# Delta-rule heads with chunks of 128 tokens: a third doubling level of the triangular inverse, half as many steps in the scan of the state

## The reference

```
G = cumsum(g, axis=-1)                                   # within a chunk
decay = exp(where(causal, G[..., :, None] - G[..., None, :], -inf))
lower = where(strict, einsum('nbhcd,nbhsd->nbhcs', kb, k) * decay, 0.0)
sol = triangular_solve(lower + eye(CHUNK), [v * beta, kb * exp(G)])
u, w = sol[..., :DV], sol[..., DV:]
qk = where(causal, einsum('nbhcd,nbhsd->nbhcs', q, k) * decay, 0.0)
q_dec, k_end = q * exp(G)[..., None], k * exp(G[..., -1:] - G)[..., None]

def step(S, inp):                                        # one chunk after another
    v_new = u - w @ S
    o = q_dec @ S + qk @ v_new
    S = exp(G[..., -1]) * S + k_end.T @ v_new
```

## Time and profile before

| | us |
|---|---|
| median of 3 runs | 1446.78 (1440.41 to 1448.28) |
| the profiled execution | 1447.03 |
| its span, first to last instruction | 1445.2 |
| PE busy | 1268.2 (88%) |
| DVE, POOL, ACT busy | 469.6, 322.9, 296.6 |
| mean granted clock of PE | 0.944 of full speed |

### The profile page before, as it was taken

One profiled execution on the slowest core, in us unless ns is written; L12 is line 12 of the kernel. 1 busy time (PEld: TensorE's weight loads), 2 busy tenths in 40 slices (PEclk: granted clock), 3 DMA queues, 4 the chain that ended last, 5 costly groups with the idle time before them and its releaser, 6 DMA issues.

```text
span 1445.2 us, 17309 instructions
## 1 busy us (share of the span) xinstructions
PE 1268.2 (88%) x5997; PEld 715.2 (49%) x5997; DVE 469.6 (32%) x1159; ACT 296.6 (21%) x619; POOL 322.9 (22%) x326
## 2 busy tenths in 40 slices
PE   3989999999997996799898879999999596989875
PEld 1447757766764754233333245666666342333223
DVE  1454555456464126000000144334342610000004
ACT  2323323332432212000010031111111310000001
POOL 0042223123121000333343102231320031323310
PEclk9989999899997997999999989999999798999997
DMA  9855535543564027999999952432410979999982
GB/s 376 338 206 199 220 92 190 199 137 144 215 221 143 24 76 318 398 375 397 380 351 387 370 211 89 128 131 92 143 60 1 388 290 380 388 396 401 424 355 106
DMA packets 91441, 351.79 MB, mean 243 GB/s; under 512 B 28997, under 2 KB 66693, under 8 KB 72464
## 3 DMA queue, kind: packets, MB, share of 16 engines
q0 software_dynamic: 19872, 188.22, 32.0%
q1 hardware_dynamic: 69280, 159.18, 30.2%
q10 hardware_dynamic: 2256, 3.96, 0.7%
HBM read 374.30 MB, written 21.60 MB: 274 GB/s over the span
## 4 chain that ended last, share of the span: by engine, by line
PE 69%; DMA 20%; DVE 5%; issue 2%; ACT 2%; POOL 1%; SPq 1%; POOLq 0%; DVEq 0%; ACTq 0%
DMA slot<-in_w_x,widx 12%; PE bank L1340 10%; PE bank L1901 9%; PE bank L1944 8%; PE bank L712 8%; PE bank L1260 6%; PE bank L807 3%; PE bank L720 2%; PE bank L352 2%; DMA out_d<-wide,lidx 2%; DMA slot<-in_ada_w 2%; PE bank L832 2%; PE bank L769 2%; PE bank L780 2%; PE bank L428 1%
## 5 line engine op out<-in xcount | busy, mean ns | idle before, releaser
L1901 PE MATMUL bank<-slot,wide 128*64 128x512 f32 x1152 | 262.6, 613 | 37.5 <-DMA slot<-in_w_x,widx 37.5
L1901 PEld LDWEIGHTS bank<-slot,wide 128*64 128x64 f32 x1152 | 89.2, 141 | 206.1 <-issue 157.2
L1340 PE MATMUL bank<-wide,slot 128*128 128x384 f32 x512 | 169.5, 488 | 3.4 <-DMA slot<-in_mlstm_w 2.0
L1944 PE MATMUL bank<-slot,wide 128*64 128x512 f32 x608 | 138.0, 607 | 21.8 <-DMA slot<-in_w_x,widx 13.7
L1340 PEld LDWEIGHTS bank<-wide,slot 128*128 128x128 f32 x512 | 95.6, 190 | 67.3 <-DMA slot<-in_mlstm_w 2.3
L712 PE MATMUL bank<-wide,slot 128*128 128x384 f32 x384 | 126.0, 488 | 0.2 <-DMA slot<-in_gdn_w 0.2
L2056 POOL DMA_INDIRECT slot<-in_w_x,widx x98 | 98.9, 1010 | 57.9 <-POOL widx L2053 41.0
L2019 DVE TENSOR_TENSOR wide<-wide,bank 128x512 f32<-128x512 f32 x19 | 13.1, 687 | 300.7 <-PE bank L1901 300.7
L712 PEld LDWEIGHTS bank<-wide,slot 128*128 128x128 f32 x384 | 72.3, 190 | 55.5 <-issue 5.9
L1944 PEld LDWEIGHTS bank<-slot,wide 128*64 128x64 f32 x608 | 46.4, 139 | 101.3 <-issue 85.2
L1260 PE MATMUL bank<-wide,slot 128*128 128x384 f32 x256 | 87.2, 503 | 7.4 <-DMA slot<-in_w_out 6.7
(11 more groups left out here) (316 smaller groups left out, 1662.7 us busy)
## 6 DMA issues: line engine op xcount, KB each, us to landing
slot<-in_ada_w SPq DMA_DIRECT2D x24, 2048.0 KB, 13.3
slot<-in_w_x SPq DMA_DIRECT2D x12, 2048.0 KB, 19.3
slot<-in_gdn_w SPq DMA_DIRECT2D x9, 2048.0 KB, 14.5
slot<-in_mlstm_w SPq DMA_DIRECT2D x16, 1024.0 KB, 7.0
wide<-rows_d SPq DMA_DIRECT2D x32, 384.0 KB, 4.4
slot<-in_w_out SPq DMA_DIRECT2D x2, 4096.0 KB, 15.3
slot<-inverse_d SPq DMA_DIRECT2D x16, 384.0 KB, 4.1
slot<-out_d SPq DMA_DIRECT2D x6, 1024.0 KB, 7.2
```

The source lines that it names most:

```text
L1340: mm = nc.tensor.matmul(bank[:, PROJ_BANK[s], 0:T], slot[:, 0, (s * KD + k) * P:(s * KD + k + 1) * P], hnT[:, k, :], start=(k == 0), stop= ...
L1901: mm = nc.tensor.matmul(bank[lanes[lane], m, :], xgT[:, k * P + lane * CAP:k * P + (lane + 1) * CAP], w[lane][:, k, :], start=(k == 0), st ...
L1944: mm = nc.tensor.matmul(bank[lanes[lane], 5 + h, :], hidT[:, k * P + lane * CAP:k * P + (lane + 1) * CAP], w_of[W_DOWN][lane][:, k, h * 51 ...
```

## The change

Chunks become as long as a tile, 128 tokens. The sums of the gates, the decays and the masks of the triangle run over 128 tokens. The inverse gets a third level, 64 to 128 (n = 2), with a third mask tile, a third X, and one mask product more on POOL; level 1 now also updates Dm. The scan has two steps in place of four: 6 chunk steps and 4 state updates; each product takes all 128 rows of a unit. In a step, the products of the old state with the decayed queries are moved ahead of the growth of the state (they stood behind it), and the last products, of the new values with the masked scores, follow in every step. The names: NL levels, NV value steps, NS state updates for a head; `grown(ch)` has one place for a chain.

```diff
-LEVELS = 6
+LEVELS = 7
...
-        levT = slot[:, 4, 0:2 * NU * P].rearrange("p (l n) -> p l n", l=2)
-        blk = slot[0:64, 4, 1536:1792].rearrange("p (j i) -> p j i", j=BLOCK)
+        levT = slot[:, 4, 0:3 * NU * P].rearrange("p (l n) -> p l n", l=3)
+        BLK = 3 * NU * P
+        blk = slot[0:64, 4, BLK:BLK + 256].rearrange("p (j i) -> p j i", j=BLOCK)
...
-        X = [slot[:, 5, 2 * NU * P:3 * NU * P], slot[:, 1, NU * P + 5 * T:2 * NU * P + 5 * T]]
+        X = [slot[:, 5, 2 * NU * P:3 * NU * P], slot[:, 1, NU * P + 5 * T:2 * NU * P + 5 * T],
+             slot[:, 4, BLK + 832:BLK + 832 + NU * P]]
...
-            chunk_sums(step, CHUNK, V[7], V[4], V[5], V[6], V[0])
-            g_last, g_first = last_of(V[7], CHUNK)
-            choose(step, small[:, 0, :], g_last, g_first, small[:, 1, :])
+            chunk_sums(step, P, V[7], V[4], V[5], V[6], V[0])
+            g_last, g_first = last_of(V[7], P)
+            choose(step, small[:, 0, 0:NT], g_last, g_first, small[:, 1, 0:NT])
...
-        CHAINS = (("p", 0, (0, 1)), ("p", 1, (1, 0)), ("s", 0, (2, 3, 4, 5)), ("s", 1, (5, 4, 3, 2)))
+        CHAINS = (("p", 0, (0,)), ("p", 1, (0,)), ("s", 0, (1, 2)), ("s", 1, (2, 1)))
...
-            for j in range(4):
-                for ch, (_, _, cs) in enumerate(CHAINS):
-                    if j < len(cs):
-                        updates = CHAINS[ch][0] == "p" or j < 3
+            for j in range(2):
+                for ch, (kind, _, tiles) in enumerate(CHAINS):
+                    if j < len(tiles):
+                        updates = j == 0
...
-                            if n == 0:
+                            if n < NL - 1:
                                 nc.tensor.matmul(bank[:, g, half], DT[:, us], early(X[n][:, us], n, g),
                                                  start=True, stop=True)
...
-                for j in range(4):
+                def unit(ch, j):
+                    _, d, tiles = CHAINS[ch]
+                    t = tiles[j]
+                    return d, t, slice((d * NT + t) * P, (d * NT + t + 1) * P)
+
+                for j in range(2):
                     now = [x for x in STEPS if x[1] == j]
                     for ch, _, v, _ in now:
...
                         if j > 0:
-                            pe.wait_ge(g_ssb, h * 10 + STATE_AT[(ch, j - 1)] + 1)
-                        nc.tensor.matmul(bank[r:r + CHUNK, *values_at(d, t)],
-                                         nwT[:, (d * NT + t) * P + r:(d * NT + t) * P + r + CHUNK], S, start=False,
+                            pe.wait_ge(g_ssb, h * NS + STATE_AT[(ch, j - 1)] + 1)
+                        nc.tensor.matmul(bank[:, *values_at(d, t)], nwT[:, us], S, start=False,
                                          stop=True, skip_group_check=True).then_inc(g_vps, 1)
                     for ch, _, v, s in now:
...
-                        pe.wait_ge(g_vsb, h * 12 + v + 1)
+                        d, t, us = unit(ch, j)
+                        S = state_of(ch, j)
+                        if S is not None:
+                            mm = into_output(S, qdT[:, us], t)
+                    for ch, _, v, s in now:
+                        d, t, us = unit(ch, j)
+                        pe.wait_ge(g_vsb, h * NV + v + 1)
                         if s is not None:
-                            nc.tensor.matmul(grown(ch, j), kend[r:r + CHUNK, u * P:(u + 1) * P],
-                                             vnew[r:r + CHUNK, u * P:(u + 1) * P], start=False, stop=True,
+                            nc.tensor.matmul(grown(ch), kend[:, us], vnew[:, us], start=False, stop=True,
                                              skip_group_check=True).then_inc(g_sps, 1)
                     for ch, _, v, s in now:
...
-                        if S is not None:
-                            mm = into_output(S, qdT[:, d * T + c * CHUNK:d * T + (c + 1) * CHUNK], c * CHUNK, (c + 1) * CHUNK)
-                        if j % 2 == 1:
-                            mm = into_output(vnew[:, u * P:(u + 1) * P], AT[:, u * P:(u + 1) * P],
-                                             (c // 2) * P, (c // 2 + 1) * P)
+                        d, t, us = unit(ch, j)
+                        mm = into_output(vnew[:, us], AT[:, us], t)
                 mm.then_inc(g_o, 1)
-                pe.wait_ge(g_ssb, h * 10 + 10)
+                pe.wait_ge(g_ssb, h * NS + NS)
...
-                    nc.scalar.activation(vnew[r:r + CHUNK, u * P:(u + 1) * P],
-                                         bank[r:r + CHUNK, *values_at(d, c // 2)], ACT.Copy).then_inc(g_vsb, 1)
+                    nc.scalar.activation(vnew[:, (d * NT + t) * P:(d * NT + t + 1) * P], bank[:, *values_at(d, t)],
+                                         ACT.Copy).then_inc(g_vsb, 1)
...
-                        if n == 0:
+                        if n < NL - 1:
                             cells = early(Dm[:, gs], n, g)
                             nc.vector.tensor_tensor(cells, cells, packed(g, n), ALU.subtract)
...
-                nc.gpsimd.tensor_tensor(em4, em4, incl.rearrange("p d (o i) -> p d o i", o=1)
+                nc.gpsimd.tensor_tensor(em4, em4, incl_tile.rearrange("p d (o i) -> p d o i", o=1)
...
-                sp.dma_start(dst.rearrange("a k d v -> (a k) d v"), Sp[:, :, 1, :]).then_inc(g_stored, 16)
+                sp.dma_start(dst.rearrange("a k d v -> (a k) d v"), Sp[:, :, 0, :]).then_inc(g_stored, 16)
```

More of the change, by code:

```diff
@@ L760, in inverse @@
                 pe.wait_ge(g_tok, h + 1)
-                for n in range(LEVELS - FIRST_LEVEL):
-                    pe.wait_ge(g_lev, h * 2 + n + 1)
+                for n in range(NL):
+                    pe.wait_ge(g_lev, h * NL + n + 1)
                     for g in range(N_DIR):
                         if n > 0:
-                            pe.wait_ge(g_inv, h * 4 + g + 1)
+                            pe.wait_ge(g_inv, h * 2 * NL + 2 * (n - 1) + g + 1)
                         for t in range(NT):
@@ L804, in scan, with into_output @@
                 first = [True]
-                def into_output(lhsT, rhs, lo, hi):
-                    mm = nc.tensor.matmul(bank[:, out_bank, lo:hi], lhsT, rhs, start=first[0], stop=False,
+                def into_output(lhsT, rhs, t):
+                    mm = nc.tensor.matmul(bank[:, out_bank, t * P:(t + 1) * P], lhsT, rhs, start=first[0], stop=False,
                                           skip_group_check=True)
@@ L930, in rest @@
             def rest(h, more, out_bank):
-                for n in range(LEVELS - FIRST_LEVEL):
+                for n in range(NL):
                     for g in range(N_DIR):
-                        act.wait_ge(g_ips, h * 8 + 4 * n + g + 1)
+                        act.wait_ge(g_ips, h * 4 * NL + 4 * n + g + 1)
                         nc.scalar.activation(early(X[n][:, g * T:(g + 1) * T], n, g), packed(4 + g, n),
@@ L944, in rest @@
                 for ch, j, v, _ in STEPS:
[L945 to L948, removed]
[L949 to L950 removed]
+                    _, d, tiles = CHAINS[ch]
+                    t = tiles[j]
+                    act.wait_ge(g_vps, h * NV + v + 1)
+                    nc.scalar.activation(vnew[:, (d * NT + t) * P:(d * NT + t + 1) * P], bank[:, *values_at(d, t)],
+                                         ACT.Copy).then_inc(g_vsb, 1)
                 act.wait_ge(g_o, h * 2 + 1)
@@ L1062, in levels @@
             def levels(h):
-                for n in range(LEVELS - FIRST_LEVEL):
+                for n in range(NL):
                     for g in range(N_DIR):
                         gs = slice(g * T, (g + 1) * T)
-                        dve.wait_ge(g_ips, h * 8 + 4 * n + 2 + g + 1)
-                        if n == 0:
+                        dve.wait_ge(g_ips, h * 4 * NL + 4 * n + 2 + g + 1)
+                        if n < NL - 1:
                             cells = early(Dm[:, gs], n, g)
@@ L1083, in states @@
                         continue
[L1084 to L1089, removed]
+                    kind, d, tiles = CHAINS[ch]
+                    t = tiles[j]
+                    dve.wait_ge(g_sps, h * NS + s + 1)
+                    src = grown(ch)
                     old = state_of(ch, j)
                     if old is None:
-                        nc.vector.tensor_copy(new, src).then_inc(g_ssb, 1)
+                        nc.vector.tensor_copy(Sp[:, d, j, :], src).then_inc(g_ssb, 1)
                     else:
[L1094 to L1099, removed]
+                        end = d * T + (t * P + P - 1 if d == 0 else t * P)
+                        dve.wait_ge(g_state, h * 16 + 16)
+                        nc.vector.scalar_tensor_tensor(out=Ss[:, d, j + 1, :], in0=old, scalar=decay_b[:, end:end + 1],
+                                                       in1=src, op0=ALU.mult, op1=ALU.add).then_inc(g_ssb, 1)
             def output(h, out_bank):
```

39 lines of the change are left out of this document (14 added, 25 removed).

## The result

The changed kernel takes 1460.1 us (median of 4 runs, 1459.6 to 1463.7), the kernel before, run beside it, 1445.0 (4 runs, 1440.4 to 1448.3). The ratio is 1.0119, with an interval from 1.0087 to 1.0151: **slower by 1.2%**, where 1.0% faster was forecast. The profiled execution has a span of 1458.4 us and a mean granted clock of 0.926 (before: 1445.2 and 0.944).

The account below looks back on a forecast made before the run. PE work was taken to bound the eight-head stage. (6.2 saved in the scan - 4.28 added in the inverse) x 8 = 15.4 us less, 0.35 more for constants: 15 us, so 1447.0 becomes about 1432 us, range 1420 to 1441.

Parts of the forecast that it names:

- The sum for undisturbed PE work: Eight heads: inverse adds 4.28 us, scan saves 6.2 us each; 15.4 us less, undisturbed heads 47.3 us apart.
- Inverse: Inverse in each head: the third level adds 4.28 us of PE work, making it 11.3 us.
- scan: Scan in each head: fewer, larger products and hidden evacuations cut 10.44 us to 4.2, a gain of 6.2.
- A fall early in the inverse: Clock dropping to half early in a head's longer inverse: priced at 9.0 us in all.
- I take nothing: POOL's third mask delaying L1171 beside DVE's block-inverse copy L1049: booked at zero, since L1049 takes 0.37 us in all heads.
- the other end: If DVE's copies wait for POOL's L1171: 1.25 us late, PE waiting in six heads, 7.5 us.
- has no idle time that was not there: Argument against early clock falls: the longer inverse continues work that kept the clock for 7 us, without new idle time.
- rival 3: Clock falls early in the longer inverse in n of eight heads: 1422 + 9.0n us; chance 0.08.
- rival 2: Scan hops not hidden or DVE late: 7.2 or 7.5 us, about 1439; both, 1447; chance 0.16.
- The prediction's case: Main case for the whole kernel: clock's cost stays as it is, about 1432 us (1427 to 1436); chance 0.56.
- Rival 1: Scan stops losing the clock and no inverse does: 9.8 us more gained, 1422 us; chance 0.15.
- The prediction's text on the clock: Half-clock stretches cost 9.8 us over six intervals; one fall of each kind, too few to price better.

Follow-up runs that it names:

- the first experiment: The changed kernel with only its third mask product on POOL moved behind DVE's block inverse: 1413.2 us, ratio 0.978 against the kernel before.
- the last: The changed kernel with all three POOL masks and the decayed queries behind DVE's block inverse: 1416.3 us, ratio 0.983 against the kernel before.

## Why the prediction was wrong

**The sum for undisturbed PE work was right.** Inverse 11.3 us forecast, 11.37 measured; scan 4.2 and 4.20; interval 47.3 and 47.30 in the first head, where PE doesn't wait ahead of L361, and 47.3 to 47.65 in the kernels without the collision and with the new order in the scan. L1008 takes 544 to 553 ns, as forecast. A fall early in the inverse was priced at 9.0 us and measured 57.6 - 48.4 = 9.2.

**The step that failed is the one on POOL: "I take nothing".** It saw the place, the instruction and the 1.25 us (copies at 401.78, L1171 until 403.0), put 7.5 us at the other end, and chose zero because L1049 took 0.37 us in all eight heads. But those eight had all begun behind POOL's last product, so they were no evidence on a copy that begins inside one. Measured, the copy takes 1.25 to 1.98 us, 0.9 to 1.6 us more than alone, and heads that keep the clock come 48.4 instead of 47.3 us apart. The 1.25 us that the prediction put at the other end was itself too long by its own rows: L1171 at 398.98 with one more mask of 1.82 ahead ends at 402.6, 0.84 us behind the copy's start. The blocking itself is as the Trainium skill says (SBUF — State Buffer, "Who interferes with whom"), in the passage that the prediction weighed and didn't follow; this trace agrees, with 0.37 us alone and 1.25 to 1.98 beside POOL.

**The second step that failed is "has no idle time that was not there".** The price of rival 3 was right and its chance, 0.08, rested on that clause. It treated the contention of rival 2 and the clock of rival 3 as separate cases. They are one: the late copy makes the late gate, which makes PE idle around its 4-column products, which is where the clock falls. The slack was in the trace of before: L359 stood 0.38 to 0.60 us behind the end of L905, 0.46 in this head.

```profile
420.21 0.47 ACT L905 ACTIVATE wide<-bank 128x384 f32<-128x384 f32 x1
421.14 0.95 PE L359 MATMUL bank<-const,ada_rows 128*128 128x4 f32 x8
```

A microsecond more on DVE uses that up and leaves about 0.5 us of waiting. The clause was also too strong as a reason: two inverses with no wait ahead of them fell, one of them in before. With four falls rival 3's own formula gives 1458, close to the measured 1460, but partly by luck: it left out the contention, and its base of 1422 stands 9 us above the 1413 of the first experiment.

The account of the six intervals closes with these two: 6 x 47.3 = 283.8; five heads with 1.1 us of contention, 5.5; three falls at 9.2, 27.6; together 316.9, as measured. The prediction's case had 283.8 and the 9.8 us that the clock cost before. The first projection 1 us later, and the last heads, with the fourth fall, 2 us longer, make up the rest of the 14.7.

Rival 1 came true once the mask was out of the way: the scan of the first experiment loses no clock in those intervals, nor does its inverse, and 1413 us stands below its 1422. The prediction's text on the clock counts one fall of each kind among six intervals; its rows hold two of the scan's kind (52.58 and 50.99 us between projections), as its rival 1 says.

**Left open:** why heads with the same wait differ, and why two inverses fell without one. In the changed kernel 0.64 us at 280.18 brought no fall and 0.51 us at 222.46 did. The Trainium skill (TensorE: Matmul & The Clock Gate, Part 1) says of the rise at a kernel's start that the same kernel makes it after a different number of products from run to run; no run here tests whether the falls differ for the same reason.

## What to carry to other kernels

Before adding a product to a lightly loaded GpSimd, look at which DVE instructions begin inside its new end, one-source copies included, and follow their lateness through ACT's queue to TensorE; here the answer was to put it behind DVE's chain of small steps. Price half a microsecond of TensorE idle time ahead of a stretch of narrow products by what the whole stretch costs at half clock, not by itself: in the changed kernel some 0.5 us ahead of the inverse cost 9.2 in four heads of six. Where narrow and wide products take the same time, try the wide ones: here they kept the clock through such a wait in six heads of six.

## What the runs showed of the hardware

- A one-source DVE copy of 24x256 fp32 that began inside a GpSimd product of two SBUF tiles ended only behind it: 0.37 us became 1.25, in one case 1.98.
- TensorE at 1.2 GHz stayed there through 20 us in which it was busy without a pause: 16 us with 64-column fp32 products (to 184.70 us) and 4 us with 128-column ones. The clock rose only within the latter (0.50 until 188 us, 0.90 from 188 to 192).
- The same stretch, behind a wait of 0.48 us, kept 2.4 GHz with 128 moving columns. A pair of instructions started every 0.22 us with 64 columns and with 128 (L777 and L779 at 2.4 GHz).
- Kernels in which TensorE had no idle time between 100 and 420 us (the first experiment and the last) lost no clock there, with the same 64-column products.
